# Dilated attention heads with tokens in fours: two small groups share one weight tile

## The reference, cut to what matters

```
h = rmsnorm(x, norm_g);  proj = h @ w_in
y_a = gated short convolution over tokens (3 taps)
y_b = causal attention of 8 heads (keys and queries of 96), gated
y_c = dilated attention, gated:
      8 heads of 64; each head has three groups g with its own q, k, v:
      g=0: dilation 1,  token i sees i-j for j <= 128
      g=1: dilation 4,  token i sees only tokens of the same residue modulo 4
      g=2: dilation 16, token i sees only tokens of the same residue modulo 16
      score = q.k / 8 - slope[g, head] * distance
      o_c = softmax over the keys of all three groups together, times their values
x = x + (g_a*(y_a @ w_a) + g_b*(y_b @ w_b) + g_c*(y_c @ w_c)) @ w_o
```

## Time and profile before

| | |
|---|---|
| median of three runs | 1452.4 us |
| profiled execution, span from first to last instruction | 1450.8 us |
| PE busy, share of the span | 1435.9 us, 99% |
| DVE, ACT, POOL busy | 72%, 58%, 6% |
| granted TensorE clock over the span | 0.999 |

### The profile page before, as it was taken

How to read it: one execution, slowest core, us unless ns; L and a number is a source line. 1 busy time by engine, 2 the same in 40 slices (tenths; PEclk the granted TensorE clock), 3 DMA queues, 4 the chain that set the end, 5 groups by cost and what they waited for, 6 DMA issues and landing times.

```text
span 1450.8 us, 30291 instructions
## 1 busy us (share of the span) xinstructions
PE 1435.9 (99%) x11628; PEld 1365.4 (94%) x11628; DVE 1043.7 (72%) x1861; ACT 848.5 (58%) x1482; POOL 90.1 (6%) x136
## 2 busy tenths in 40 slices
PE   8999999999999999999999999999999999999999
PEld 6888999999979999999998989999999898999999
DVE  2878898888776668855666857876676684787664
ACT  4566666555556756445576766555566676656543
POOL 0111011110000000000020000320000000031000
PEclk9999999999999999999999999999999999999999
DMA  9966799996674366766663554336666355434663
GB/s 362 337 213 218 240 325 348 338 346 224 201 235 157 117 214 193 221 198 191 194 233 113 173 167 146 97 129 189 194 194 208 113 171 170 143 98 130 189 202 118
DMA packets 81186, 292.06 MB, mean 201 GB/s; under 512 B 9185, under 2 KB 10465, under 8 KB 80946
## 3 DMA queue, kind: packets, MB, share of 16 engines
q1 hardware_dynamic: 68274, 244.31, 51.8%
q0 software_dynamic: 11792, 42.77, 8.8%
q10 hardware_dynamic: 1008, 3.41, 0.7%
HBM read 289.40 MB, written 1.05 MB: 200 GB/s over the span
## 4 chain that ended last, share of the span: by engine, by line
PE 88%; DVE 7%; ACT 3%; issue 2%; DMA 1%; SPq 0%; DVEq 0%; ACTq 0%
PE G L513 22%; PE G L514 22%; PE G L515 22%; DVE wlo L1697 2%; PE G L572 2%; PE G L574 2%; PE G L573 2%; ACT whi L1177 1%; PE O L1120 1%; PE Tp L966 1%; PE Tp L908 1%; PE S L1019 1%; DVE aw L1705 1%; PE S L1089 1%; PE Tp L1044 1%
## 5 line engine op out<-in xcount | busy, mean ns | idle before, releaser
L1697 DVE TENSOR_TENSOR wlo<-raw,whi 128x1024 fp32r<-128x1024 f32 x444 | 545.9, 1232 | 253.8 <-ACT whi L1177 252.1
L1177 ACT ACTIVATE whi<-raw 128x1024 fp32r<-128x1024 f32 x444 | 468.7, 1058 | 217.8 <-PE G L515 157.4
L513 PE MATMUL G<-h,whi 128*128 128x256 f32 x2064 | 582.2, 282 | 0.3 <-DVE wlo L1697 0.2
L514 PE MATMUL G<-h,whi 128*128 128x256 f32 x2064 | 571.1, 277 | 0.0
L515 PE MATMUL G<-h,wlo 128*128 128x256 f32 x2064 | 571.0, 277 | 0.0
L513 PEld LDWEIGHTS G<-h,whi 128*128 128x128 f32 x2064 | 387.9, 188 | 5.6 <-issue 2.6
L514 PEld LDWEIGHTS G<-h,whi 128*128 128x128 f32 x2064 | 387.9, 188 | 0.7 <-issue 0.5
L515 PEld LDWEIGHTS G<-h,wlo 128*128 128x128 f32 x2064 | 387.7, 188 | 0.0
L1705 DVE CUSTOM_DVE_ANT_0 aw<-aw,cs,cols 128x1024 f32<-128x1024 f32 x80 | 101.4, 1279 | 0.0
L513 PE MATMUL G<-ah,whi 128*128 128x256 f32 x352 | 97.2, 276 | 0.0
L514 PE MATMUL G<-ah,whi 128*128 128x256 f32 x352 | 97.2, 276 | 0.0
(11 more groups left out here) (419 smaller groups left out, 2332.9 us busy)
## 6 DMA issues: line engine op xcount, KB each, us to landing
raw<-in_w SPq DMA_DIRECT2D x444, 512.0 KB, 4.0
aw<-in_ada POOLq DMA_DIRECT2D x80, 512.0 KB, 5.3
adaw<-in_ada SPq DMA_DIRECT2D x8, 1024.0 KB, 15.6
sn<-in_uq ACTq DMA_DIRECT2D x2, 768.0 KB, 4.4
x<-in_x SPq DMA_DIRECT2D x1, 1024.0 KB, 5.5
pt<-in_ukv ACTq DMA_DIRECT2D x2, 512.0 KB, 5.5
out<-x SPq DMA_DIRECT2D x4, 256.0 KB, 2.3
dec<-in_dec ACTq DMA_DIRECT2D x1, 512.0 KB, 7.2
```

Of the source, the lines that this page charges most:

```text
L513: pe.matmul(o, wh, mv[:, 0:T], start=(k == 0), stop=False)
L514: pe.matmul(o, wh, mv[:, T:2 * T], start=False, stop=False)
L1177: act.activation(whi[:, s, :], raw[:, s, :], ACT.Copy).then_inc(w_hi, 1)
L1697: dve.tensor_tensor(wlo[:, s, :], raw[:, s, :], whi[:, s, :], ALU.subtract).then_inc(w_lo, 1)
```

## The change

The token order is now by residue modulo 4: column 64r + i holds token 4i + r. It is set once, in `norm_tiles`, which reads `x` through `by_four` (step of four elements), so that every projection of `h` comes out in this order. What needs natural order (the convolution's input, the causal heads' output, the residual) is converted where it is written. In this order groups 1 and 2 need only four 64x64 tiles each on the diagonal of their 256x256 score matrices. The two tiles of group 1 for a query tile of 128 go onto the diagonal of one 128x128 tile and those of group 2 onto its other two quarters. So one softmax-weight tile for 128 queries serves both small groups, and a head has 768 columns instead of 1024.

- `dil_scores`: first the two 128x256 instructions of group 0, then eight 64x64 instructions of the small groups (64-row contraction, 64 queries, 64 keys).
- `minima`: two groups with two instructions each (512 and 256 columns in all) instead of three with six in all. The spans of ACT's exponentials and DVE's divisions are 384 columns instead of 512.
- `to_keys`: six transposes instead of eight, copied by ACT as 256 and 512 columns.
- Values: the values of group 1 and group 2 are stacked on the two halves of the partitions of `dv`, by ACT (`values_out`, 512 columns by 64 partitions instead of 256 by 128). For group 2 the value projection (j from 8 on) takes its weights for one half from `hy`, a copy of `h` in another order that POOL makes with four copies for each layer.
- `pair_outs`: the group 0 part is as before; the small groups take eight instructions with 64 streamed columns instead of eight with 128.
- POOL's bias for a head: one instruction of 512 columns and two of 128.

```
-WEIGHT_TILES = ((256, 768, 384, 896), (0, 512, 128, 640))
+WEIGHT_TILES = ((256, 640), (0, 384, 128, 512))
...
-    return (slice(0, 512), slice(512, 1024)) if i >= 8 else (slice(0, P), slice(P, 384))
+    return (slice(0, 384), slice(384, 768)) if i >= 8 else (slice(0, P), slice(P, 384))
...
+def by_four(ap):
+    return ap.rearrange("p (i r) -> p r i", r=4)
+def in_fours(ap):
+    return ap.rearrange("p (r i) -> p r i", r=4)
...
+                pool.wait_ge(blk_done, B_HYB + H_DQ + 7 + l * HYB_BLOCKS)
+                pool.wait_ge(h_ready, 40 + l * 8)
+                for c, o in ((0, 192), (64, 0), (128, T + 192), (192, T)):
+                    ins = pool.tensor_copy(hy[:, :, c:c + 64], h[:, :, o:o + 64])
+                ins.then_inc(hy_ready, 1)
...
-                        if by_parity:
-                            hh, hl = even_odd(h[:, k, 0:T])[:, tt, :], even_odd(h[:, k, T:2 * T])[:, tt, :]
+                        if crossed:
+                            hh, hl = (h[:, k, o + 64:o + 192] for o in (0, T)) if tt == 0 else \
+                                (hy[:, k, o:o + P] for o in (0, P))
...
-                    for grp, qt in ((1, 0), (0, 0), (1, 1), (0, 1), (2, 0), (2, 1)):
-                        if qt == 0:
-                            slots[grp] = use_s()
-                        t, o = places[grp]
-                        tile = slice(qt * P, (qt + 1) * P)
-                        ins = pe.matmul(S[:, slots[grp], PLACES[grp][qt][0]], dqk[o:o + 64, t, tile],
-                                        dqk[o:o + 64, 12 + t, tile if grp else slice(0, T)], start=True, stop=True)
-                        if qt:
-                            ins.then_inc(s_done, 1)
+                    slots = [use_s(), use_s()]
+                    for qt in range(2):
+                        ins = pe.matmul(S[:, slots[0], PLACES[0][qt][0]], dqk[far:far + 64, 3 * p + 2 * e, qt * P:qt * P + P],
+                                        dqk[far:far + 64, 12 + 3 * p + 2 * e, 0:T], start=True, stop=True)
+                    ins.then_inc(s_done, 1)
+                    for qt in range(2):
+                        for t, swap in ((3 * p + e, 0), (3 * p + 1 + e, 1)):
+                            for a_ in range(2):
+                                q0, c = qt * P + 64 * a_, qt * P + 64 * (a_ ^ swap)
+                                keys = dqk[near:near + 64, 12 + t, q0:q0 + 64]
+                                ins = pe.matmul(S[64 * a_:64 * a_ + 64, slots[1], c:c + 64],
+                                                dqk[near:near + 64, t, q0:q0 + 64], keys, start=True, stop=True)
+                    ins.then_inc(s_done, 1)
...
+                    for n in range(4 if last >= 8 else 0):
+                        for e in range(2):
+                            i = 2 * p + e - 8
+                            c = 512 + 512 * (n % 2) + 64 * i
+                            ins = pe.matmul(O[64 * e:64 * e + 64, 64 * n:64 * n + 64], dv[:, n // 2, c:c + 64],
+                                            pt2[:, e, 64 * n:64 * n + 64], start=False, stop=(n == 3))
...
-                        dve.scalar_tensor_tensor(out=sq[:, k, :], in0=x[:, k, :], scalar=entry_gain(l, k), in1=rstd[:, :],
-                                                 op0=ALU.mult, op1=ALU.mult).then_inc(t_ready, 1)
+                        dve.scalar_tensor_tensor(out=in_fours(sq[:, k, :]), in0=by_four(x[:, k, :]),
+                                                 scalar=entry_gain(l, k), in1=by_four(rstd[:, :]), op0=ALU.mult,
+                                                 op1=ALU.mult).then_inc(t_ready, 1)
```

More of the change, by code:

```diff
@@ L480, in _ @@
             pool.wait_ge(in_hyb, 64)
[L481 to L489, removed]
-                                       ALU.mult).then_inc(bias_ready, 1)
+            for l in range(LAYERS2):
+                pool.wait_ge(blk_done, B_HYB + H_DQ + 7 + l * HYB_BLOCKS)
[3 more added lines that the diff above has]
+                ins.then_inc(hy_ready, 1)
+                for head in range(8):
+                    taken_s = L1_S + l * HYB_S + (score_uses(7 + head) if head else 1)
+                    pool.wait_ge(s_free, taken_s - 1)
+                    pool.tensor_tensor(bias[:, 0:512], dist[:, 0:512], slopes[:, head:head + 1].broadcast_to([P, 512]),
+                                       ALU.mult).then_inc(bias_ready, 1)
+                    if head:
+                        pool.wait_ge(s_free, taken_s)
+                    far, near = (t[:, 512:768].rearrange("p (q c i) -> p q c i", q=2, c=2) for t in (bias, dist))
+                    for c in range(2):
+                        n = 8 + 8 * c + head
+                        pool.tensor_tensor(far[:, :, c, :], near[:, :, c, :],
+                                           slopes[:, n:n + 1].unsqueeze(2).broadcast_to([P, 2, 64]),
+                                           ALU.mult).then_inc(bias_ready, 1)
         @block.tensor
@@ L1592, in _, with values_out @@
                         qk_across(j - 19)
+                def values_out(grp, tt):
+                    g = G_HYB + H_DV + 4 * grp
+                    if grp == 0:
+                        evac_tokens(g, dv[:, :, 0:512], tt)
+                        return
+                    for half in range(2):
+                        n, r = 2 * half + tt, slice(64 * half, 64 * half + 64)
+                        kt, c = (tt, 512 + 512 * half) if grp == 1 else (half ^ tt, 1024 - 512 * half)
+                        act.activation(dv[r, kt, c:c + 512], G[r, (g + n) % 2, :], ACT.Copy)\
+                           .then_inc(slot_free[(g + n) % 4], 1)
                 for j in range(12):
@@ L2458, in tables, with near @@
     t["sbm"] = np.where(k2[None, :] + r[:, None] < q2[None, :], 0, -MASKED).astype(f)
-    q = np.arange(T).reshape(P, 2).T
-    far = q[:, :, None] - q.reshape(-1)[None, None, :]
-    near = [np.where((far >= 0) & (far % d == 0) & (far // d <= back), far, MASKED) for d, back in zip(DIL, N_BACK)]
-    t["dist"] = np.concatenate([near[0][0], near[0][1]] + [near[g][n][:, n * P:(n + 1) * P] for g in (1, 2) for n in range(2)],
-                               axis=1).astype(f)
-    t["slopes"] = np.tile(np.array(SLOPES, f)[None, :], (P, 1))
+    q = np.arange(T).reshape(64, 4).T.reshape(2, 2, 64)
+    rows_, own = q.reshape(2, P), np.stack([q, q[:, ::-1]]).reshape(2, 2, P)
+    def near(far, d, back):
+        return np.where((far >= 0) & (far % d == 0) & (far // d <= back), far, MASKED)
+    wide = [near(rows_[e][:, None] - q.reshape(-1)[None, :], DIL[0], N_BACK[0]) for e in range(2)]
+    half = r[:, None] // 64 == r[None, :] // 64
+    both = [np.where(half, near(rows_[e][:, None] - own[0, e][None, :], DIL[1], N_BACK[1]),
+                     near(rows_[e][:, None] - own[1, e][None, :], DIL[2], N_BACK[2])) for e in range(2)]
+    t["dist"] = np.concatenate(wide + both, axis=1).astype(f)
+    steep = np.array(SLOPES, f).reshape(3, 8)
+    low = np.broadcast_to(r[:, None] < 64, (P, 8))
+    t["slopes"] = np.concatenate([np.tile(steep[0], (P, 1)), np.where(low, steep[1], steep[2]),
+                                  np.where(low, steep[2], steep[1])], axis=1).astype(f)
     t["bones"] = np.kron(np.eye(2), np.ones((64, 64))).astype(f)
```

108 lines of the change are left out of this document (52 added, 56 removed).

## The result

The changed kernel takes 1464.01 us (median, 1463.97 to 1464.63), against 1451.93 us for the kernel before in the same session. The ratio is 1.0084, with a 95% interval from 1.0072 to 1.0096: slower by 12 us. The forecast was 1453.2 us and its range ended at 1460.5: the time lies beyond it. The profiled execution has a span of 1462.2 us, 11.4 us more than before, at the same granted clock of 0.999.

A forecast was written before the change was run, and what follows sets the result against it. PE's own stream was taken to set the end. Scores +9.3, transposes -3.4, products -3.5, value projection -0.8 and the wait -0.8 summed to +0.8 us on 1452.4, giving 1453.2 us, range 1448.5 to 1460.5.

The forecast's parts named there:

- What bounds the kernel now: Whole kernel: PE's own stream sets the end; less work on DVE, ACT or POOL is worth at most 0.8 us.
- Scores: Dilated heads on PE: lost overlap and one more shape change, 0.58 us a head over 16 heads, +9.3 us.
- products: Dilated pairs on PE: eight small-group passes of 64 columns instead of 128, 0.43 us a pair, -3.5 us.
- transposes: Dilated heads on PE: six instead of eight, 0.106 us each, -3.4 us.
- the wait: PE's 0.76 us wait at the loop's end for the first layer's last tile: taken as gone, -0.8 us.
- the value projection: Value matmuls in both hybrid layers: weights no longer from every second column of `h`, 288 x 2.7 ns, -0.8 us.
- short passes don't get shorter: Rival, 15% (partly or wholly): 64-column passes in scores and products cost 0.109 us like 128-column ones; 10.5 us more, 1463.7 us.
- No drain: Rival, 10%: large and small scores overlap across 64x128 and 64x64 shapes, so 0.58 us a head vanishes; 1443.9 us.
- Steps of 16 bytes: Rival, 13%: DVE instructions of 256 columns in steps of four grow 0.27 us, making PE wait at layer entries; 1455.6 us.
- Same, 0.54: Outcome case: chance 0.54 that the time can't be told from no change, 1449.5 to 1455.3 us.

The follow-up runs named there:

- the last run: Changed kernel with the 32 bytes put back and the large group's scores, still 64x128 instructions, one ahead of and one behind the eight small ones: 1456.78 us.

## Why the prediction was wrong

**The sum.** Its terms were the instructions that the diff edits. The one term that decided was in none of its parts: `HYB_S` goes from 40 to 32, `mark` becomes 32 bytes narrower, and every tensor behind it moves. The diff shows the first step and the prediction doesn't mention it. Its sum puts the G blocks at nothing, without a reason; they cost +10.5 us, and with the 32 bytes put back 10.9 us of the time are gone (1464.01 against 1453.06).

**"What bounds the kernel now"** was right, and so the term mattered in full: PE's own stream sets the end, and the prediction even said that every nanosecond added to it counts. It applied that to the 53 us of scores, products and transposes that were edited and took the pace of the G blocks as fixed. Four ns on some 2200 matmuls of `ah`, `yh` and `oh`, and 0.3 ns on 6000 of `h`, outweigh everything that was priced.

**The parts.** Scores, products, transposes and the wait came out as priced (above), and the value projection gained 0.4 us and not 0.8. What was said of the transposes' own time (0.64 us) left out the step to the scores' tile shape behind them; their saving was right. The 0.15 us taken for the change from 64x128 to 64x64 is 0.19 by the last run. With the addresses back the kernel takes 1453.06 us against 1453.2, and there the forecast holds part by part.

**The rivals.** The time lies almost at the 1463.7 us of *short passes don't get shorter*, by accident. The small scores take 0.61 us where that rival needs 0.9, and the products got shorter by what was forecast. *No drain* is refuted for two shapes and true for one (1.01 us). *Steps of 16 bytes* was right about the instruction (0.68 for 0.48 us, 0.20 more where it took 0.27) and wrong about its effect. The Trainium skill says that a different cacheline for each access brings a penalty (Advanced Engine Details and Errata, SBUF Cachelines), with which the 0.20 us agree in kind.

**Same, 0.54.** These chances were given to a kernel whose layout stays. No case of the forecast had a change in what isn't edited, so none of the cases reached far enough.

## What to carry to other kernels

When one engine's stream sets the end, price what an edit does to the instructions around it too: a size, a slot count or a new buffer ahead of others moves every later tensor, and whether a stream runs at 113 or 118 ns is invisible in busy shares. Compare mean durations of groups that the change does not touch first; if they differ, put the addresses back with an unused buffer before explaining anything else. Concurrent products in different halves of the rows should have one tile shape, even if that doubles the instructions.

## What the runs showed of the hardware that was not expected

- The pace of float32 products of rounded operands (128x128 weights, 256 columns, a load for each) depends on the distance between the first bytes of the streamed tensor and of the weight tile, modulo 128: by long stretches, 64 gives 113.3 ns at best, 32 gives 117.2 to 118.9, 96 gives 118.0 to 118.6, and 0 gives 118.3 to 120.2. Other distances weren't tried, nor was a cause inside the memory. The Trainium skill says that the two reads have ports of their own and that loading weights does not steal bandwidth from the running matmul (TensorE: Matmul & The Clock Gate, Step-by-step: what each phase is for); here the stream's pace changes by 3 to 6% with the distance between what the two read, so they are not independent of each other.
- At the good distance a stream has a second pace, 117.8 ns, taken in its first matmuls and kept, for up to 1000 of them. What decides is open. It cost 12 us in the run that moved everything by 64 bytes, and 4 us through one stretch of `h` in the run that moved `ah` alone. The five executions of the kernel before that took some 8 us longer than the rest may have the same cause; none of them was profiled, so this isn't shown.
- A 64-column pass takes 0.61 us less the 0.15 to 0.19 of the shape change, over 8: 53 to 58 ns, half that of a 128-column one.
